# A state-space mixer unrolled over its head pairs, its group root moved onto the output products, and linear attention's gates placed under those products

## The reference

```
h = rms_norm(x);  proj = h @ w_in        # z, xbc, dt, q, k, v, g, gk_low
# state-space mixer, 16 heads of 64 in 2 groups, chunks of 128 tokens
xbc = silu(conv4(xbc) + b);  xs, B, C = split(xbc);  dt = softplus(dt + dt_bias)
a_cum = cumsum(-exp(a_log) * dt) per chunk
y = (C B^T * exp(a_cum_l - a_cum_s), l >= s) @ (xs*dt)      # y_diag
  + exp(a_cum_l) * C @ prev_state + xs * d_skip             # y_off, skip
y = rms_norm(y * silu(z), per group of 512 features) * norm_w
# linear attention, 4 heads, chunks of 64 tokens
gk = log_sigmoid(gk_low @ w2 + b) / 16;  gcum = cumsum(gk) per chunk
x = x + concat(y, o_gla) @ w_out
```

## Time and profile before

| | us |
|---|---|
| three runs, median (lowest to highest) | 3178.92 (3175.0 to 3183.72) |
| profiled execution | 3174.49 |
| its span | 3172.7 |
| busy PE / POOL / DVE / ACT | 2992.0 / 1814.5 / 1197.0 / 553.2 |
| mean granted TensorE clock | 0.972 |

### The profile page before, as it was taken

The page is one execution under the profiler, slowest core; times in us unless marked ns, Lnnn a source line. Parts: engine busy times, 40 slices in busy tenths (PEclk is TensorE's granted clock), DMA queues, the critical chain, the costliest instruction groups (busy, mean ns, idle before and its releaser), DMA issues.

```text
span 3172.7 us, 37079 instructions
## 1 busy us (share of the span) xinstructions
PE 2992.0 (94%) x13766; PEld 2389.5 (75%) x13766; DVE 1197.0 (38%) x1485; ACT 553.2 (17%) x725; POOL 1814.5 (57%) x1822
## 2 busy tenths in 40 slices
PE   5867899899999899999999999999999999999999
PEld 3645687788887567788887778868888777788887
DVE  4445222433243556442333211233324265544131
ACT  2222121210001244200001110121000244410000
POOL 4213354477777223576776546547777643477775
PEclk8878899899999899999999999999999999999999
DMA  3101121122323000122223212112222211122322
GB/s 122 40 27 40 57 80 67 40 94 89 103 88 102 32 30 27 67 93 99 93 90 109 80 66 93 66 67 93 90 102 89 100 40 59 53 93 87 105 89 90
DMA packets 37371, 242.05 MB, mean 76 GB/s; under 512 B 4144, under 2 KB 4272, under 8 KB 15280
## 3 DMA queue, kind: packets, MB, share of 16 engines
q1 hardware_dynamic: 36288, 237.19, 21.9%
q10 hardware_dynamic: 1008, 3.83, 0.4%
HBM read 238.90 MB, written 2.10 MB: 76 GB/s over the span
## 4 chain that ended last, share of the span: by engine, by line
PE 89%; DVE 5%; ACT 1%; issue 1%; DVEq 1%; POOL 1%; DMA 1%; ACTq 0%; SPq 0%; POOLq 0%
PE ps L391 60%; PE ps L413 12%; PE ps L1184 1%; PE ps L1153 1%; PE ps L979 1%; PE ps L1116 1%; PE ps L996 1%; PE ps L1006 1%; POOL w_lo L647 1%; PE ps L1170 1%; PE ps L1197 1%; DVE scr L1694 1%; PE ps L785 1%; PE ps L1102 1%; DVE a_lo L1604 1%
## 5 line engine op out<-in xcount | busy, mean ns | idle before, releaser
L643 POOL CAST w_hi<-raw 128x512 fp32r<-128x512 f32 (+1 forms) x909 | 578.0, 678 | 1320.7 <-PE ps L391 923.3
L647 POOL TENSOR_TENSOR w_lo<-raw,w_hi 128x512 fp32r<-128x512 f32 (+1 forms) x909 | 1236.5, 1390 | 20.2
L391 PE MATMUL ps<-h_hi,w_hi 128*128 128x512 f32 (+1 forms) x1928 | 765.1, 397 | 34.3 <-DVE scr L1793 15.4
L391 PE MATMUL ps<-h_lo,w_hi 128*128 128x512 f32 (+1 forms) x1928 | 756.1, 392 | 0.0
L391 PE MATMUL ps<-h_hi,w_lo 128*128 128x512 f32 (+1 forms) x1928 | 755.0, 392 | 0.0
L391 PEld LDWEIGHTS ps<-h_hi,w_hi 128*128 128x128 f32 (+1 forms) x1928 | 365.3, 189 | 126.5 <-issue 29.2
L391 PEld LDWEIGHTS ps<-h_lo,w_hi 128*128 128x128 f32 (+1 forms) x1928 | 365.0, 189 | 77.3 <-issue 2.9
L391 PEld LDWEIGHTS ps<-h_hi,w_lo 128*128 128x128 f32 (+1 forms) x1928 | 364.6, 189 | 77.8 <-issue 0.7
L391 PE MATMUL ps<-a_hi,w_hi 128*128 128x512 f32 x752 | 293.0, 390 | 1.8 <-DVE a_lo L1604 1.8
L391 PE MATMUL ps<-a_lo,w_hi 128*128 128x512 f32 x752 | 292.6, 389 | 0.0
L391 PE MATMUL ps<-a_hi,w_lo 128*128 128x512 f32 x752 | 292.5, 389 | 0.0
(11 more groups left out here) (261 smaller groups left out, 3679.8 us busy)
## 6 DMA issues: line engine op xcount, KB each, us to landing
raw<-weights SPq DMA_DIRECT2D x169, 1024.0 KB, 4.8
raw<-weights SPq DMA_DIRECT2D x64, 704.0 KB, 4.1
raw<-weights SPq DMA_DIRECT2D x8, 640.0 KB, 3.9
raw<-weights SPq DMA_DIRECT2D x8, 512.0 KB, 3.6
x<-x_in SPq DMA_DIRECT2D x1, 2048.0 KB, 8.9
x_out<-x SPq DMA_DIRECT2D x1, 2048.0 KB, 6.3
scr<-phase_ret ACTq DMA_DIRECT2D x1, 1536.0 KB, 8.4
scr<-phase_mla ACTq DMA_DIRECT2D x1, 640.0 KB, 4.2
```

The costliest lines, as they stand in the source:

```text
L391: mm = pe.matmul(out_ap, a, b, start=(i == 0 and not begun), stop=(i == n - 1 and ended))
L643: ins = pool.tensor_copy(w_hi[:, slot, piece], raw[:, slot, piece])
L647: ins = pool.tensor_tensor(w_lo[:, slot, piece], raw[:, slot, piece], w_hi[:, slot, piece].bitcast(F32), ALU.subtract)
```

## The change

- The loop over groups becomes a straight program over eight pairs; no buffer is shared between group end and group start.
- dt's and B's products are interleaved by tile of h. The first conv tap goes to ACT.
- Running sums are split into high and low and spread by PE with a broadcast column of the identity; the causal mask is added in PSUM by eight identity-times-mask products a pair; ACT takes exp(sum - own sum) of 128 columns at a time, the own sum as its bias. DVE's row, clip and C-scaling operations go. The exponential of the spread sums multiplies y_off on DVE after the product, so y_from_states uses C directly.
- y is split without the root: ACT writes high, DVE low and adds the squares. The root multiplies each half of each output tile on DVE (`ssd_residual`).
- The first norm's squares are summed by eight products on PE, not by DVE.
- Gates' products stand before the output products, their logarithm and sums beside them; head 0's q and k take the last pair's place for projections, and the chunk stream is reordered accordingly. The phase transfer of linear attention is merged into the first one.
- Linear attention's last head has 36 output products between its steps.

```diff
+                for k in (0, KD - 2, KD - 1) if n else range(KD):          # PE, norm
...
+                for k in range(KD):                                        # PE, ssd: dt and B
+                    pe.wait_ge(*ready[k])
...
+                chunk_split(c0 + 2)
+                features(pe, ps[:, 4, :], c0 % 2, 256, 0, P)
+                features(pe, ps[:, 5, :], c0 % 2, 256, P, P).then_inc(s_used, 1)
...
+                def segments(u):
+                    for e in range(2):
+                        k = 2 * u + e
+                        if u:
+                            pe.wait_ge(s_ex, k - 1)
+                        sel = r_ident[0:16, k:k + 1].to_broadcast([16, P])
+                        for i, part in enumerate((c_hi, c_lo)):
+                            pe.matmul(ps[:, 4 + e, :], sel, part, start=(i == 0), stop=False, skip_group_check=True)
+                        for tb in range(TB):
+                            mm = pe.matmul(ps[:, 4 + e, tb * P:(tb + 1) * P], r_ident, r_mask, start=False, stop=True,
+                                           skip_group_check=True)
+                        mm.then_inc(s_bc, 1)
+
+                def sums_spread(u):
...
+                    for e in range(2):
+                        sel = ident[0:16, 2 * u + e:2 * u + e + 1].to_broadcast([16, 64])
+                        mm = pe.matmul(ps[64 * e:64 * e + 64, 7, :], sel, d_cum[0:16, :], start=True, stop=True)
+                    mm.then_inc(s_eb, 1)
...
+                def y_diag(u):
+                    pe.wait_ge(s_hm, 2 * u + 2)
+                    if u:
+                        pe.wait_ge(s_y, u)
                     for tb in range(TB):
                         s = slice(tb * P, (tb + 1) * P)
+                        for e in range(2):
+                            r = slice(64 * e, 64 * e + 64)
+                            pe.matmul(ps[r, 6, s], xdt[:, tb, r], head_e[:, e, s], start=True, stop=True)
+
+                def y_from_states(u):
                     pe.wait_ge(s_prev, u + 1)
+                    pe.wait_ge(s_ea, u + 1)
+                    for tb in range(1, TB):
                         s = slice(tb * P, (tb + 1) * P)
+                        mm = pe.matmul(ps[:, 7, s], prev[:, tb - 1, :], cm_t[:, u // 4, s], start=True, stop=True)
+                    mm.then_inc(s_yy, 1)
+
+                segments(0)
+                sums_spread(0)
+                for u in range(8):
+                    turn_x(u)
+                    if u < 7:
+                        proj_x(u + 1)
+                    else:
+                        proj_qk(0, 0)
+                        proj_qk(0, 1)
+                    states(u)
+                    y_diag(u)
+                    if u == 5:
+                        group_mean(0, 4)
+                    if u < 7:
+                        proj_z(u + 1, 0)
+                    else:
+                        proj_qk(1, 0)
+                    y_from_states(u)
+                    if u < 7:
+                        proj_z(u + 1, 1)
+                        if u == 5:
+                            pe.wait_ge(s_gr2, 1)
+                        segments(u + 1)
+                        sums_spread(u + 1)
+                    else:
+                        proj_qk(1, 1)
...
+            def ssd_residual(c0):
+                pe.wait_ge(s_y, 8)
+                for hh, bank in enumerate((6, 7, 2, 3)):
+                    mm = pe.matmul(ps[:, bank, :], param("gk_w2", hh * P, P)[0:16, :], d_gk[0:16, :], start=True, stop=True)
+                mm.then_inc(s_gk, 1)
+                pe.wait_ge(s_ex, 16)
+                for t in range(KD):
+                    if t % 2 == 0:
+                        chunk_split(c0 + t // 2)
+                    if t == 1:
+                        pe.wait_ge(s_gab, 1)
+                    if t == 2:
+                        pe.wait_ge(s_gr2, 2)
+                    if t > 2:
+                        pe.wait_ge(s_res, t)
+                    for g in range(2):
+                        bank = (4, 6, 2)[t % 3] + g
...
+                    if t == 0:
+                        group_mean(1, 2)
...
+                    if not ahead:                                          # PE, gla, last head
+                        pe.wait_ge(s_ggs, hd + 2)
+                        residual_begun("gla", range(4))
                     pe.wait_ge(s_gst, 4 * hd + 4)
...
+                def exps(u):                                               # ACT
+                    for e in range(2):
+                        act.wait_ge(s_bc, 2 * u + e + 1)
+                        for tb in range(TB):
+                            s = slice(tb * P, (tb + 1) * P)
+                            ins = act.activation(head_e[:, e, s], ps[:, 4 + e, s], ACT.Exp,
+                                                 bias=d_ncum[:, tb, 2 * u + e:2 * u + e + 1])
+                        ins.then_inc(s_ex, 1)
+                    act.wait_ge(s_eb, u + 1)
+                    act.activation(head_ea, ps[:, 7, :], ACT.Exp).then_inc(s_ea, 1)
...
+                for u in range(7):
+                    if u:
+                        y_out(u - 1)
+                    act.wait_ge(s_px, u + 2)
+                    conv_begun(u + 5, 1, u + 1)
+                    if u == 5:
+                        group_rstd(0, 4)
+                    conv_out(u + 5, ssd_x[:, (u + 1) % 2, :], u + 1)
+                    z_silu(u + 1)
+                    exps(u + 1)
+                y_out(6)
+                y_out(7)
+                group_rstd(1, 2)
...
+                for u in range(8):                                         # DVE
+                    x_tokens(u)
+                    decayed(u)
+                    if u:
+                        y_out(u - 1)
+                    if u < 7:
+                        conv(u + 5, 1, u + 1)
+                    states(u)
+                    gated(u)
+                y_out(7)
...
+                for t in range(KD):
+                    if t == 2:
+                        gates_summed()
...
+                    for g in range(2):
+                        dve.tensor_tensor(res_t[:, g, :], ps[:, (4, 6, 2)[t % 3] + g, :], y_rstd[:, g, :], ALU.mult)
+                    settled().tensor_tensor(res_t[:, 0, :], res_t[:, 0, :], res_t[:, 1, :], ALU.add)
+                    settled().tensor_tensor(x[:, t, :], x[:, t, :], res_t[:, 0, :], ALU.add).then_inc(s_res, 1)
```

More of the change, by code:

```diff
@@ new lines, in proj_x, with proj_z, proj_qk @@
+                def proj_x(u):
+                    chunk_split(c0 + 3 + u)
+                    if u:
+                        pe.wait_ge(s_conv, 4 + u)
+                    proj(u, 1).then_inc(s_px, 1)
+                def proj_z(u, part):
+                    if u and part == 0:
+                        pe.wait_ge(s_z, u)
+                    mm = proj(u, 0, range(4 * part, 4 * part + 4))
+                    if part == 1:
+                        mm.then_inc(s_used, 1)
+                def proj_qk(half, part):
+                    if half == 0 and part == 0:
+                        chunk_split(c0 + 11)
+                        pe.wait_ge(s_z, 8)
+                    if half == 1 and part == 0:
+                        pe.wait_ge(s_conv, 12)
+                    mm = features(pe, ps[:, half, :], (c0 + 11) % 2, 256, P * half, P, tiles=range(4 * part, 4 * part + 4))
+                    if half == 1 and part == 1:
+                        mm.then_inc(s_used, 1)
@@ new lines, in turn_x, with states @@
+                    mm.then_inc(s_xT, 1)
+                def states(u):
+                    pe.wait_ge(s_xdt, u + 1)
+                    if u:
+                        pe.wait_ge(s_prev, u)
+                    for tb in range(TB - 1):
+                        s = slice(tb * P, (tb + 1) * P)
+                        mm = pe.matmul(ps[:, 3, s], bm_tok[:, u // 4, s], xdte[:, tb, :], start=True, stop=True)
+                    mm.then_inc(s_st, 1)
+                def y_diag(u):
+                    pe.wait_ge(s_hm, 2 * u + 2)
+                    if u:
+                        pe.wait_ge(s_y, u)
@@ L840, in slot @@
+            def gla(c0):
+                c0 = c0 - 1
                 def slot(hd, r):
@@ L907, in mix @@
                     mm.then_inc(s_go, 1)
+                    if not ahead:
+                        residual_begun("gla", (4,))
                     pe.wait_ge(s_gsq, hd + 1)
@@ new lines, in ssd @@
+                wait_used(c0 + 1)
+                for n in range(2):
+                    conv_begun(n, 2 + n, 8 + n)
+                conv_out(0, b_t[0], 8)
+                wait_used(c0 + 2)
+                conv_begun(2, 4, 10)
+                conv_out(1, b_t[1], 9)
+                conv_begun(3, 5, 11)
+                for g in range(2):
+                    act.wait_ge(s_bt, g + 1)
+                    act.activation(bm_tok[:, g, :], ps[:, 2 + g, :], ACT.Copy).then_inc(s_btok, 1)
+                conv_out(2, cm_t[:, 0, :], 10)
```

488 lines of the change are left out of this document (226 added, 262 removed).

## The result

| | before | after | forecast |
|---|---|---|---|
| median, us | 3181.1 (4 runs, 3175.0 to 3183.7) | 3081.1 (4 runs, 3080.8 to 3083.0) | 3085 (3062 to 3112) |
| profiled span, us | 3172.7 | 3081.2 | 3078.5 (3172.7 - 94.2) |
| mean granted clock | 0.972 | 0.982 | |

What follows compares the result with a forecast made beforehand. TensorE, holding 89% of the chain of waits, was taken as the bound, with gains only from gaps and clock: -3 - 65.6 - 10.3 - 12.8 - 2.5 = -94 us, 3174.5 to 3080, plus 4.4 for the median: 3085 us, range 3062 to 3112.

Steps and rivals of the forecast that it cites:

- y_diag 1.9: In each pair, eight full-f32 products of 128 columns and 64 outputs, one every 0.22 us: 1.9 us with its start.
- sums_spread ... 2.0: In each pair, two full-f32 products of 512 columns at 1.05 us each: 2.0 us of TensorE work.
- second rival: Column halves overlap, so y_diag and sums_spread halve: -8 us, 3077; 3070 were the states in time too; chance 0.17.
- 0.6 us of stall: In each pair, TensorE's wait at y_from_states for VectorE's states, half of the span 0 to 1.1; pair of 20.0 us.
- first rival: VectorE sets the pair, its two-input operations held up beside Pool's split: 2.3 us more per pair, 3106; chance 0.22.
- With no gap over 1.1 us the clock should hold: In the pairs, gaps of at most 1.1 us keep TensorE's high clock; granted clock over 0.95 expected.
- segments 2.2: In each pair, four f32r products of 512 columns (0.23 each) and eight of 128 (0.15 taken): 2.2 us.
- Gates and output products ... -10.3: Stage after the pairs: 61.0 us becomes 50.7, including 2 us of stall at the third output tile.
- fourth rival: Gates aren't hidden: VectorE needs 50 us against 44 in the output products, Pool's chunk late: +9, 3094; chance 0.08.
- Setup: Before the pairs: first x transposes at 94.5 us instead of 97.5, so -3 us, bounds -8 and +5.
- squares at 0: At the very start, first norm's squares summed by eight TensorE products instead of VectorE additions: -2 to +2 us, taken as 0.
- last head's -2.5: Linear attention's last head: 36 output products moved into its waits save 2.5 us, bounds -6 and 0.

Runs made afterwards that it cites:

- halves in order: Changed kernel with a pair's eight y_diag products issued all to the lower 64 output rows, then all to the upper, instead of in turn: 3086.5 us, one run.
- full rows: Changed kernel with the products that spread running sums (pairs and gates) taking 128 rows, 112 of them zero, instead of 16: 3065.5 us.
- gates last: Changed kernel with VectorE's part of linear attention's gates after the last of eight output tiles instead of before the third: 3074.9 us.

## Why the prediction was right

The bound and the mechanism held. That the total came within 4 us is in part luck: errors of -8.7 and +5.6 us, and larger ones inside the pairs, cancelled.

- **Bound and mechanism: right.** The gain comes from TensorE's gaps. Idle time in the pairs went from 56 to 0.8 us, and 74 of the 91.5 us of the profiled gain lie there. This is read from the traces of before and after, not from an experiment on the parts.
- **"y_diag 1.9" and "sums_spread ... 2.0": too long.** 1.03 and 1.01, because the two column halves pass together (halves in order, and the start times). That is -1.9 us a pair; over the stage, with eight times y_diag and seven times sums_spread, -14. The forecast had this as its second rival at 0.17, and its mechanism was real. Its 3077 stood 4 us from the truth, but by luck: it counted states that come late, and for states in time, as they were, it named 3070; what it lacked is the clock. The rule of the Trainium skill (TensorEngine Tiling (Array Packing), Key Properties), that 64-column tiles run in parallel, agrees: products on the two halves start 0.008 us apart, 1.03 us in turn against 1.51 in order.
- **"0.6 us of stall": too much**, 0.8 us in all pairs. States were late by 0.3 us at most, but only because TensorE was slower than need be: with full rows it waited 4.5 us in five pairs, up to 1.05 us in one and 0.6 a pair in the mean, which is what the forecast had. The first rival's premise is in the trace of after (VectorE's masked scores, L1873, and the tokens' second operation, mean of 16 and of 8 instances):

```profile
L1873 DVE TENSOR_TENSOR scr<-scr 128x512 f32<-128x512 f32 x16 | 22.3, 1433 | 0.0
L1868 DVE TENSOR_TENSOR scr<-scr 128x512 f32<-128x512 f32 x8 | 8.6, 1080 | 0.6
```

  1.43 and 1.08 us against 0.68 when free, so VectorE was slower beside GpSimd as feared, in the part of a pair where it had time to spare. The Trainium skill (SBUF — State Buffer, Who interferes with whom) gives an exclusive lock on a port pair as the reason, which VectorE's operations with two SBUF inputs and GpSimd's reads share. The lengths agree with it on both sides (GpSimd's subtraction took 9.3 us beside the gates and 5.0 at its shortest in the same stage); the lock itself no run isolates.
- **"With no gap over 1.1 us the clock should hold": failed.** Mean clock 0.95, with dips behind busy stretches. The step looked for idle time only; what brought the clock down was a run of small products over 16 rows. By the pairs of the kernels: 148.2 - 135.2 = 13.0 us lost, of which 4.6 are the segments' own length (7 x 0.65), 0.8 waits, and 7.6, the remainder, the clock. The trace of after bears the remainder out: three dips of some 1.5 us each, and 2.7 us in the first pair, which began at the lower level (0.50 from 90 to 100 us) and took 20.6 us, the next one 17.9. The clock took back half of what the shorter products gave. The stage's -8.7 is then, as an estimate from these rows, -14 for the products, -3.4 for the stall (0.8 for 4.2), +2.1 for the segments, +7.5 for the clock and -1 for the last pair (14.15 us, forecast 16.0 with y_diag at 1.9). The mean pitch of the first seven pairs was 19.1 us, between the forecast's 20 and its second rival's 18 to 19.
- **"segments 2.2": 2.5**, since the four products of 512 columns had been priced by rows where all products have 128 rows; over 16 rows, among products over 128, they take 0.33 each.
- **"Gates and output products ... -10.3": -4.7.** The stall at the third tile was forecast at 2 us and came (2.87, VectorE). Missing were GpSimd's chunk under the gates (1.45), the low clock behind it (1.8) and behind the gates' 16-row products (7.2 for the first tile, where 24 products at 0.227 are 5.4, so 1.7). The gates' products took 3.6 us of the 4.2 forecast. The fourth rival had VectorE's and GpSimd's parts; gates last showed them, with the low clock behind them, to be 5.3 us.
- **"Setup": right in its parts** (7.7 of 7.8, 4.4 of 4.7), and the -3 within what repeats: 96.6 and 94.3 in two executions of one kernel. The squares at 0: -1.3 to -2.6 at the first dt product; at the first x transposes one experiment gave no more than the setup's own variation and the other 3.3 to 3.5 us, so the term was put too low, by 1 to 3 us.
- **Linear attention: right** (22.4 of 22.3). The last head's -2.5 is undecided; the experiment gave 0.6 to 1.0.

## What to carry to other kernels

Where TensorE is busy but small products stand in the loop, price each by a row of its own shape, rows of the contraction included, and look at the granted clock behind them: padding the contraction with zeros to all 128 rows, as the products around them have, made this stretch shorter and kept the clock, 9 us in eight pairs for two memsets. Ask of each long VectorE burst beside GpSimd's work which of GpSimd's transfers to TensorE it stretches, and put it where that split has slack. And when a loop's pacer is made faster, read the loop again: the next wait, 4.6 us in five pairs here, went by changing the order of two steps, though only 1 to 2 us of it can be seen in the whole time.

## What was not expected of the hardware

- The granted clock fell from 1.00 to 0.52 behind 3.5 us in which TensorE was busy throughout, with products over 16 rows; over 128 rows, same columns, it stayed at 1.00 for 139.5 us. Three of seven such runs of products were followed by a dip, and none in six executions over 128 rows. In the setup the same products didn't bring it back either: it was at 0.50 from 90 to 100 us.
- Where f32r products of 512 columns over 16 rows stand among products over 128, each took 0.33 us to the next start and four 128-row products of 128 columns behind them 0.59; with 128 rows throughout it was 0.23 and 0.40, all at clock 1.00. In a row of full-f32 products the number of rows made no difference (0.43 us an instruction in the gates).
- Eight full-f32 products onto 64 output rows took 1.03 us with the halves in turn, both halves stepping together at 0.218 us a product; sent one half after the other they still overlapped in part and took 1.51.
- GpSimd's subtraction for a chunk took 4.9 us at its shortest, 5.8 beside VectorE's output tiles, 9.3 beside the long operations on the gates.
- Identical instructions of four heads took 228.6 to 237.3 us from kernel to kernel, by the granted clock of stretches that contain waits. A gain of under 5 us elsewhere can't be read from the whole span of one execution.
